# GpSimd multiplies rows by a factor with TENSOR_SCALAR in place of TENSOR_TENSOR over a broadcast operand

## The reference

```
# differential attention, 4 heads, per block of 128 queries (16 blocks)
sc = einsum('bqhmd,bkhmd->bmhqk', qb, k) * scale + bias      # two score maps m = 0, 1
p = softmax(sc, axis=-1)
a = p[:, 0] - lam * p[:, 1]                                   # lam: one learned number of the layer
o = einsum('bhqk,bkhd->bqhd', a, v)

# attention over neighbours, 6 heads, each block sees itself and its two neighbours
p = exp(sc - m)
p = p / (sum(p, axis=-1) + exp(sink - m))
o = einsum('bngrqk,bnkgd->bnqgrd', p, v)
```

## Time and profile before

| | |
|---|---|
| median of three runs | 4088.17 us |
| the profiled execution's own time | 4092.34 us |
| span of its trace | 4090.5 us |
| PE busy | 3788.4 us, 93% |
| GpSimd (POOL) busy | 2488.2 us, 61% |
| DVE busy | 2234.5 us, 55% |
| ACT busy | 1657.8 us, 41% |
| mean granted TensorE clock | 0.977 |

### The profile page before, as it was taken

The page is one execution under the profiler, slowest core; times in us unless marked ns, Lnnn a source line. Parts: engine busy times, 40 slices in busy tenths (PEclk is TensorE's granted clock), DMA queues, the critical chain, the costliest instruction groups (busy, mean ns, idle before and its releaser), DMA issues. The chain is left out here.

```text
span 4090.5 us, 51527 instructions
## 1 busy us (share of the span) xinstructions
PE 3788.4 (93%) x19002; PEld 2626.4 (64%) x19002; DVE 2234.5 (55%) x3991; ACT 1657.8 (41%) x2882; POOL 2488.2 (61%) x1393
## 2 busy tenths in 40 slices
PE   8999999999989899789889999999999898997898
PEld 8788774555546565558787897755555465655587
DVE  3012135555569999675430021255555699996754
ACT  3112104333358888661031121033333588886610
POOL 1221326877769999755512213277777699997555
PEclk9999999999989999999989999999999899999999
DMA  5333534342220222325353335323322202223353
GB/s 178 124 138 117 169 115 109 78 101 64 57 56 1 56 56 52 91 83 184 130 177 124 129 120 152 130 57 75 75 65 57 56 1 56 56 52 90 88 181 129
DMA packets 179680, 391.38 MB, mean 96 GB/s; under 512 B 17854, under 2 KB 98984, under 8 KB 167784
## 3 DMA queue, kind: packets, MB, share of 16 engines
q1 hardware_dynamic: 178568, 386.70, 33.9%
q10 hardware_dynamic: 864, 1.41, 0.2%
HBM read 254.88 MB, written 135.67 MB: 95 GB/s over the span
## 5 line engine op out<-in xcount | busy, mean ns | idle before, releaser
L1279 POOL TENSOR_TENSOR mla_sum_pool<-mla_sum_pool,mla_probs 128x1024 f32<-128x1024 f32 (+1 forms) x336 | 777.9, 2315 | 207.0 <-ACT mla_probs L1240 182.2
L1297 DVE TENSOR_REDUCE carry_row_max<-psum 128x1 f32<-128x512 f32 x688 | 474.4, 690 | 413.6 <-PE psum L1112 409.1
L1240 ACT ACTIVATE mla_probs<-psum 128x1024 f32<-128x1024 f32 x384 | 373.3, 1021 | 693.6 <-PE psum L1149 686.4
L1545 ACT ACTIVATE diff_probs<-psum,diff_shift 128x1024 f32<-128x1024 f32 x512 | 566.1, 1111 | 195.3 <-DVE diff_shift L1620 189.7
L1613 DVE TENSOR_REDUCE diff_row_max<-psum 128x1 f32<-128x1024 f32 x512 | 612.5, 1218 | 52.5 <-PE psum L1480 38.3
L1492 PE MATMUL psum<-ident,diff_probs 128*128 128x128 f32 x2048 | 329.8, 284 | 107.1 <-DVE diff_turned L1647 72.6
L624 PE MATMUL psum<-in_x_hi,in_w_hi 128*128 128x512 f32 x1024 | 404.5, 395 | 2.7 <-ACT in_mla_val L733 2.7
L624 PE MATMUL psum<-carry_firsts,in_w_hi 128*128 128x512 f32 x1024 | 404.8, 395 | 0.0
L624 PE MATMUL psum<-in_x_hi,in_w_lo 128*128 128x512 f32 x1024 | 401.6, 392 | 0.0
L1492 PEld LDWEIGHTS psum<-ident,diff_probs 128*128 128x128 f32 x2048 | 215.8, 141 | 285.5 <-issue 188.5
L1162 PE MATMUL psum<-mla_probs,mla_v_op 128*64 128x512 f32 x1536 | 373.1, 607 | 0.0
(11 more groups left out here) (206 smaller groups left out, 7369.1 us busy)
## 6 DMA issues: line engine op xcount, KB each, us to landing
in_w_raw<-in_w_in SPq DMA_DIRECT2D x64, 512.0 KB, 3.9
split_d<-in_out SPq DMA_DIRECT2D x64, 512.0 KB, 2.6
raw_d<-in_out SPq DMA_DIRECT2D x32, 512.0 KB, 2.6
mq_d<-in_out SPq DMA_DIRECT2D x48, 256.0 KB, 3.4
mk_d<-in_out SPq DMA_DIRECT2D x48, 256.0 KB, 3.8
carry_firsts<-split_d SPq DMA_DIRECT2D x48, 256.0 KB, 7.9
carry_weights<-split_d SPq DMA_DIRECT2D x48, 256.0 KB, 7.7
carry_weights<-split_d SPq DMA_DIRECT2D x16, 768.0 KB, 17.7
```

Source lines behind the costliest of these rows:

```text
L1240: nc.scalar.activation(probs[:, s % RING, :].rearrange("p (a n) -> p a n", n=CH), psum[:, S0 + 2 * (s % 2):S0 + 2 * (s % 2) + 2, :], ACT.E ...
L1279: nc.gpsimd.tensor_tensor(acc, start, probs[:, s % RING, mine], ALU.add).then_inc(pool_added, 1)
L1297: nc.vector.tensor_reduce(row_max[:, u % 2, qb, n:n + 1], psum[:, sweep_bank(g), :], AX.X, ALU.max).then_inc(maxed, 1)
L1545: nc.scalar.activation(dst[:, half * HALF:(half + 1) * HALF].rearrange("p (a n) -> p a n", n=CH), banks(n, m, half), ACT.Exp, bias=shift[: ...
```

## The change

Three multiplications on GpSimd are written with another instruction. `tensor_tensor` reads two tensors, the second one here a single column that an access pattern with step 0 spreads over the row. `tensor_scalar` reads one tensor, and takes the factor as one number per partition. The places, the sizes, the results, the semaphores and the order stay as they are.

```
-                    nc.gpsimd.tensor_tensor(second, second, ratio[:, n % 2:n % 2 + 1].broadcast_to([P, HALF - CH]),
-                                            ALU.mult).then_inc(times_ratio, 1)
+                    nc.gpsimd.tensor_scalar(second, second, ratio[:, n % 2:n % 2 + 1], None, ALU.mult
+                                            ).then_inc(times_ratio, 1)
...
-                    nc.gpsimd.tensor_tensor(third, third, ratio[:, n % 2:n % 2 + 1].broadcast_to([P, HALF]), ALU.mult
+                    nc.gpsimd.tensor_scalar(third, third, ratio[:, n % 2:n % 2 + 1], None, ALU.mult
                                             ).then_inc(times_ratio, 1)
...
-                        nc.gpsimd.tensor_tensor(row, row, inv[:, qb % 2, h:h + 1].broadcast_to([P, w]), ALU.mult
+                        nc.gpsimd.tensor_scalar(row, row, inv[:, qb % 2, h:h + 1], None, ALU.mult
                                                 ).then_inc(scaled, 1)
```

## The result

The changed kernel took 4289.05 us, median of 4 runs (4282.33 to 4290.22), against 4089.43 for the kernel before (the three times of above and a fourth): 1.048 times as long, 95% interval 1.0464 to 1.0495. The forecast was 4074, the range ended at 4185. The change costs 200 us.

What follows compares the result with a forecast made beforehand. POOL was taken to set the mean pace of the differential stages. Gains of 10.0 us in the units and 4.1 at the stage ends, together 14, took 4088.17 to 4074; the range was 4066 to 4185.

Steps and rivals of the forecast that it cites:

- What bounds the kernel: Differential stages: POOL sets the mean pace, 7.82 us a unit, but costs time only in five or six units a head.
- The price of TENSOR_SCALAR: POOL's products: priced like the CAST, 1.04 us for 1024 columns and about 0.6 for 512, making a unit 6.5 us.
- The dear end of the range: POOL's products at the price of the two-tensor rows: a unit grows by 0.73 us, 93 us in all, 4181.
- Rival 1: POOL's units: TENSOR_SCALAR slower than the broadcast form, 93 us more at two-tensor prices; chance 0.36, of which 0.18 above 4185.
- The gain of a faster POOL: Differential stages: 10.0 us saved in the units and 4.1 at the ends of both stages, together 14 us.
- Rival 3: Units 18 to 24: TENSOR_SCALAR fast, but other engines hold them near 7.8 us; gain 4 to 8 us, chance 0.08.
- The pace of 7.55 us: Differential stages, band in the first half of the row: the other engines' step for a unit once POOL is faster.
- The likeliest case: Whole kernel: 4068 to 4084 us, from a gain of 5 us at least and 19 at most.
- The attention over neighbours: Its blocks: POOL has slack, 4.75 us of 7.46, so the change counts as nothing there.
- The library load: Before the first TENSOR_SCALAR: hidden in POOL's idle time ahead of L1593, 22 us in each stage; cost nothing.

Runs made afterwards that it cites:

- e2: Only the product of 512 columns (L1593) written as TENSOR_SCALAR, against the kernel before: 4162.46 us, ratio 1.0172.
- e3: Only the product of 1024 columns (L1599) written as TENSOR_SCALAR, against the kernel before: 4213.47 us, ratio 1.0299.
- e1: Kernel before with a block ahead in which GpSimd runs each instruction form six times: one-operation TENSOR_SCALAR 2.842 us for 1024 columns, multiply and add 1.192.
- e6: All three products as TENSOR_SCALAR with both operations filled (times the factor, plus 0.0), against the kernel before: 4078.21 us, ratio 0.9972.
- e4: Only the products of the attention over neighbours (L1821) written as TENSOR_SCALAR, against the kernel before: 4095.32 us, ratio 1.0016.

## Why the prediction was wrong

- **What bounds the kernel: right.** POOL was the mean pace with no slack to spare. Each 0.1 us more in a unit costs 12.8 us: e2 (0.524 us in a unit) was to cost 67 us and cost 64 to 77, e3 (0.955 us) was to cost 122 and cost 116 to 128.
- **The price of TENSOR_SCALAR: wrong, and this is the step that failed.** "Price falls with what is read, and the new form reads one stream. I therefore take the row of the CAST": 1.04 us for 1024 columns, measured 2.851; about 0.6 for 512, measured 1.567. The rows bore out the rule for a copy and for TENSOR_TENSOR. Nothing in them said that it holds for TENSOR_SCALAR with an empty second place, and e1 shows that it doesn't: 2.84 us alone and in a row, with one stream read, against 1.04 for the copy, 1.89 and 2.34 for the two TENSOR_TENSOR forms. The pairs of multiply and add take 1.118 us for 1024 columns and 0.692 for 512, or 0.83 ns a column; the form of the change takes 2.5. The Trainium skill (GPSIMD Engine Reference, § Performance versus the Vector engine) has 1.03 cycles an element for a loop of at most two operations, from which the prediction made an estimate of 0.88 us for 1024 columns, 0.86 ns each. The pairs agree with that, and for the form of the change the measurement decides against it.
- **The dear end of the range: wrong too.** The two-tensor row was taken as the dearest plain one, which gave 4181. The nearest row by operands was no bound for another instruction. It wasn't the dearest plain row of the trace either, for an addition of 1024 columns in the output projection has a mean of 3.231:

```profile
L2213 POOL TENSOR_TENSOR early_w_raw<-early_w_raw,out_b_row 128x1024 f32<-128x1024 f32 x32 | 103.4, 3231 | 2.5
```

  That mean hides two prices: 14 of the 32 take 4.30 to 4.33 us, the other 18 take 2.34 to 2.40. The 14 are just those that run beside DVE's TENSOR_TENSOR of 2048 columns at L2257, for 2.07 us of their time. In the differential stages POOL's additions of the same size keep to 2.35 to 2.39 us.

  Rival 1 did say that nothing in the trace ends the case at 0.73 us, and the chance of 0.18 above 4185 is where it came out: 1.48 us in a unit are 189 us, measured 191 in the two stages.
- **The gain of a faster POOL: right, with another instruction.** 10 us in the units and 4 at the ends were forecast; e6 has 11 (7 to 16), its two stages are 12.5 us shorter, and the two stretches that were forecast came out within 0.1 us. Some of that closeness is luck, since single steps missed both ways: 7.86 us for the 7.75, 7.79 for the 7.93, and 7.64 and 7.44 in turn for the 7.55. Rival 3 (4 to 8 us) is not shut out by the interval alone, but the stretches follow the forecast. The pace of 7.55 us was there to be had. The likeliest case was given as 4068 to 4084, where its own bounds of 5 and 19 us give 4069 to 4083, and rival 3's 4 to 8 us lie wholly within the 0.2% of which the text gives it half; neither slip moves the verdict.
- **The attention over neighbours: cost put at nothing.** Six products at 7.46 us took away all of POOL's slack, also in the first blocks, which had come faster than 7.46; the two stages are 8 us longer, and e4 alone costs 2 to 10.
- **The library load: right.** Its row, of POOL's sequencer after, stands 12.8 us ahead of the first product (1191.30), while POOL waited for the ratio anyway. In e1, where nothing hides it, the row stands at 2.5 to 2.6 us, the first TENSOR_SCALAR starts at 2.71, and all six take 2.837 to 2.850 us, so no cost of the load shows there either:

```profile
L1593 POOLq MODIFY_POOL_CONFIG  x2: 11/11/11, 1178.5 to 1178.6; - x2
```

## What to carry to other kernels

An instruction that the trace doesn't have can't be priced here by what it reads and writes: on GpSimd, forms over the same 1024 columns took from 1.04 to 3.78 us, and the dearest read one tensor. Measure it by itself, six in a row, before it goes into the pace-setting queue; a run of that kind settled the price in this case. If a tile is to be multiplied by a factor per row there, fill both places of the TENSOR_SCALAR (times the factor, plus 0.0): 1.12 us for 1024 columns, against 1.90 for the broadcast form and 2.85 with the second place empty. And an engine that is the pace by a little, with others close behind, loses in full when it gets slower and wins little when it gets faster: here 128 us for each us in a unit one way, and 11 us in all the other way (7 to 16).

## What the runs showed of the hardware that was not expected

- TENSOR_SCALAR on GpSimd, float32, 128 x 1024: one operation 2.84 us, multiply and add in any of the three orders tried 1.12 with one factor from a tile, 1.19 with two and 1.04 with constants (both measured for multiply and add), the two other pairs tried 3.7 and 3.8.
- The broadcast TENSOR_TENSOR (1.892 us) is cheaper than the two-tensor one (2.338), though both take two operands.
- The same TENSOR_TENSOR addition of 1024 columns (L2213, kernel before) takes 2.34 to 2.40 us, and 4.30 to 4.33 in each of the 14 cases where it runs beside DVE's TENSOR_TENSOR of L2257. Why, no run here shows.
- The prices in the probe and in the differential stage, beside DVE and ACT at work, differ by less than 2% (2.842 and 2.851, 1.892 and 1.896, 2.338 and 2.375 us).
